# Ten instead of eight k-tiles of a hidden chunk through seven block products, their combinations seeded in PSUM

## The chip, the cores and the metric

The kernel runs on one core of one Trainium2 chip. A time is the device time of an execution in microseconds, and the median of several executions counts. The chip has five engines that matter here: TensorE (PE, matmuls), VectorE (DVE), ScalarE (ACT), GpSimd (POOL) and SyncE (SP, which issues most DMAs).

## What is computed

One layer of an encoder for 256 positions of width 2048: a half-step SwiGLU FFN, a combined attention of 16 heads with input and output projection, and a second half-step FFN. Only the first matrix product of the two FFNs is touched by the change:

```python
D_MODEL, SEQ, D_FF = 2048, 256, 5632

def swiglu_ffn(x, g, w_in, w_out):
    h = rms_norm(x, g)
    gate, up = jnp.split(h @ w_in, 2, axis=-1)
    return (jax.nn.silu(gate) * up) @ w_out

x = x + 0.5 * swiglu_ffn(x, ffn1_norm, ffn1_w_in, ffn1_w_out)
...
x = x + 0.5 * swiglu_ffn(x, ffn2_norm, ffn2_w_in, ffn2_w_out)
```

All data are float32, and the result has to be near float32.

## The kernel before

**Matmuls.** A float32 operand is split into a high part, rounded by ACT (`w_hi`, `h_hi`), and a low part, the rest, made by DVE (`w_lo`, `h_lo`). A product then takes three matmuls of 128 x 128 by 128 x 512: hi hi, hi lo, lo hi. Positions come in two tiles t of 128, the width 2048 in 16 k-tiles, the hidden width 5632 in 11 chunks of 512 (`NC`). Each chunk needs a gate and an up half of the weights.

**Units and the ring.** Weights land in `w_raw` (four slots of four k-tiles) or in the blocks `b_11`, `b_12`, `b_21`, `b_22`. They are used in units of two k-tiles (`UK`). Unit u is rounded by ACT into `w_hi[u % 4]` (`split_in_hi`, L963, counter `hi_ready`), DVE makes `w_lo[u % 4]` from it (`split_in_lo`, L1338, `lo_ready`), PE uses both (`units_used`). ACT waits for PE to be through with unit u-4 (`RING` = 4). ACT and DVE take their instructions in the order of the program, and so do their other duties, which are written out by hand between the units.

**Chunks.** The first chunk is computed plainly (16 units, gate in `acc[0]`, up in `acc[1]`). For the other ten (`IN_LOOPS`), 8 of the 16 k-tiles (`K_PLAIN`) are computed plainly and 8 through block products. The blocks are 2 x 2: the weights' k-tiles 8 to 11 and 12 to 15 by gate and up (`b_11`, `b_12`; `b_21`, `b_22`), the activations' position tiles by the same k-tiles. Seven products of 4 k-tiles (`KS`) take the place of eight:

- P1 = first activation block by `b_11`, P2 = second by `b_21`, P4 by the full sum `b_21` + `t_1`, P3 = fourth activation sum by `b_22`
- P5, P6 by `t_1` (the first sum `b_12 + b_11`, then the second sum `b_22 + t_1`), P7 by `b_12` after the third sum (`b_22 + b_12`)

DVE makes the three weight sums (`weight_sum`, L1353) and a DMA of POOL that accumulates adds `t_1` to `b_21` (L1909). The sums of the activations are made once per FFN (`activation_wide`, `signed_sums`, `split_sums`). P1, P6 and P7 go to the PSUM bank `partial[0]`, P5 to `partial[1]`. ACT copies P1 to `rows` (L1007), DVE adds P6, P7 and P5 there (L1411, L1447, L1449), and at the end of a loop adds the rows to `acc[0]` and `acc[1]` (L1411) before SiLU (L1047) and the gate product (L1465).

**Order of a loop on PE** (`hidden`): gate units G0, G0, G1, G1; eight transposes of the previous chunk's result (L570), which ACT copies to `act_raw` (L1012); P1, P5, an up unit, P2, an up unit, P6, P3, P7, P4, two up units. In all 8 plain units of 12 matmuls and 14 product units of 6. The loops are hardware loops over pairs of chunks on PE, ACT, DVE and SP (the last pair is written out on ACT and DVE).

**Beginning of the kernel.** SP issues x, the first chunk's weights, the blocks of the next one, a plain piece G0, then 17 small constants, then the other pieces. DVE runs `lambda_sums` (L1731 to L1733), which waits for these constants, behind the low parts of the first loop's G0 and G1 units, and after it the gate product of the first chunk (L1557).

## Time and profile before

| | us |
|---|---|
| median of 3 runs | 1803.63 (1803.62 to 1804.79) |
| the profiled execution | 1803.53 |
| its span in the profile | 1801.7 |
| PE, DVE, ACT busy | 1796.4, 1509.1, 1071.0 |

A row of the profile names engine, line, operation, output and inputs by the program's names. Times of a timeline count from the start of the span. A matmul's end is modelled, so that following matmuls overlap; their starts give the rate. SPq, PEld: the DMA issues of SyncE, the weight loads of TensorE.

### The profile page before, as it was taken

The page shows a single profiled execution, that of the slowest core. Times are in us where ns is not written, and L with a number is a line of the kernel's source. Part 1 is how long each engine was busy: PE and PEld are TensorE (multiplying, and loading weights), DVE is VectorE, ACT ScalarE, POOL GpSimd, SP SyncE. Part 2 cuts the span into 40 slices and gives each one's busy share as a digit, 9 for nine tenths or more (in the row PEclk, how much of TensorE's full clock was granted, in tenths as well). Part 3 has the DMA queues.
Part 4 walks back from the last instruction along what each step waited for, and adds up shares of the span by engine and source line. Part 5 has one row for each costly group of instructions (what it writes and reads, how often), then busy time and mean ns, then how long its engine had stood idle before and what let it go on. Part 6 is the DMA issues. An engine that isn't in the chain of part 4 may idle for free.

```text
span 1801.7 us, 22755 instructions
## 1 busy us (share of the span) xinstructions
PE 1796.4 (100%) x8227; PEld 1491.4 (83%) x8227; DVE 1509.1 (84%) x1594; ACT 1071.0 (59%) x1295; POOL 60.7 (3%) x93
## 2 busy tenths in 40 slices
PE   9999999999999999999999999999999999999999
...
PEclk9999999999999999999999999999999999999999
...
GB/s 359 235 238 233 234 230 210 221 222 186 164 169 251 188 220 212 197 171 164 164 164 187 143 166 182 257 222 224 235 238 240 227 232 237 127 187 164 238 206 141
DMA packets 181286, 372.92 MB, mean 207 GB/s; under 512 B 7504, under 2 KB 8544, under 8 KB 178400
## 3 DMA queue, kind: packets, MB, share of 16 engines
...
## 4 chain that ended last, share of the span: by engine, by line
PE 100%; DVE 0%; ACT 0%; POOL 0%; issue 0%; ACTq 0%; POOLq 0%
PE acc L539 14%; PE acc L541 14%; PE acc L540 13%; PE acc L601 8%; PE acc L599 8%; PE acc L600 8%; PE turn L612 4%; PE turn L613 4%; PE turn L614 4%; PE acc L612 3%; PE acc L614 3%; PE acc L613 3%; PE turn L570 1%; PE turn L716 1%; PE turn L715 1%; PE turn L714 1%
## 5 line engine op out<-in xcount | busy, mean ns | idle before, releaser
L1327 DVE TENSOR_TENSOR w_lo<-w_raw,w_hi 128x1024 fp32r<-128x1024 f32 x167 | 205.1, 1238 | 132.6 <-ACT w_hi L944 132.1
L944 ACT ACTIVATE w_hi<-w_raw 128x1024 fp32r<-128x1024 f32 x166 | 175.4, 1059 | 198.7 <-PE acc L541 177.1
L963 ACT ACTIVATE w_hi<-b 128x1024 fp32r<-128x1024 f32 x200 | 212.5, 1063 | 117.9 <-PE acc L601 76.1
L1338 DVE TENSOR_TENSOR w_lo<-b,w_hi 128x1024 fp32r<-128x1024 f32 x200 | 240.7, 1221 | 35.3 <-ACT w_hi L963 29.8
L977 ACT ACTIVATE w_hi<-w_raw 128x1024 fp32r<-128x1024 f32 x176 | 185.2, 1058 | 121.1 <-PE acc L541 87.8
L601 PE MATMUL acc<-w_hi,h_lo 128*128 128x512 f32 x640 | 249.1, 389 | 0.0
L599 PE MATMUL acc<-w_hi,h_hi 128*128 128x512 f32 x640 | 249.0, 389 | 0.0
L600 PE MATMUL acc<-w_lo,h_hi 128*128 128x512 f32 x640 | 249.0, 389 | 0.0
L1348 DVE TENSOR_TENSOR w_lo<-w_raw,w_hi 128x1024 fp32r<-128x1024 f32 x176 | 213.0, 1222 | 32.1 <-ACT w_hi L977 28.7
L963 ACT ACTIVATE w_hi<-w_raw 128x1024 fp32r<-128x1024 f32 x160 | 169.5, 1061 | 91.6 <-PE acc L601 64.1
L1338 DVE TENSOR_TENSOR w_lo<-w_raw,w_hi 128x1024 fp32r<-128x1024 f32 x160 | 191.9, 1220 | 28.8 <-ACT w_hi L963 26.2
L539 PE MATMUL acc<-w_hi,h_hi 128*128 128x512 f32 x496 | 196.4, 396 | 0.0
L541 PE MATMUL acc<-w_hi,h_lo 128*128 128x512 f32 x496 | 193.2, 390 | 0.0
L540 PE MATMUL acc<-w_lo,h_hi 128*128 128x512 f32 x496 | 193.1, 389 | 0.0
L539 PE MATMUL acc<-w_hi,act_hi 128*128 128x512 f32 x480 | 187.1, 390 | 0.0
L541 PE MATMUL acc<-w_hi,act_lo 128*128 128x512 f32 x480 | 186.8, 389 | 0.0
L540 PE MATMUL acc<-w_lo,act_hi 128*128 128x512 f32 x480 | 186.7, 389 | 0.0
L963 ACT ACTIVATE w_hi<-t 128x1024 fp32r<-128x1024 f32 x80 | 85.0, 1062 | 104.0 <-PE acc L601 98.1
L599 PEld LDWEIGHTS acc<-w_hi,h_hi 128*128 128x128 f32 x640 | 120.1, 188 | 25.1 <-DVE w_lo L1338 0.3
L601 PEld LDWEIGHTS acc<-w_hi,h_lo 128*128 128x128 f32 x640 | 120.1, 188 | 25.0
L600 PEld LDWEIGHTS acc<-w_lo,h_hi 128*128 128x128 f32 x640 | 120.1, 188 | 24.9
L539 PEld LDWEIGHTS acc<-w_hi,h_hi 128*128 128x128 f32 x496 | 93.1, 188 | 21.2 <-issue 2.7
...
## 6 DMA issues: line engine op xcount, KB each, us to landing
w_raw<-in_ffn_w_in SPq DMA_DIRECT2D x94, 1024.0 KB, 5.1
w_raw<-in_ffn_w_out SPq DMA_DIRECT2D x88, 1024.0 KB, 5.2
b<-in_ffn_w_in SPq DMA_DIRECT2D x80, 1024.0 KB, 5.3
w_raw<-in_w_in SPq DMA_DIRECT2D x48, 1024.0 KB, 5.0
b<-t POOLq DMA_DIRECT2D x20, 1024.0 KB, 8.3
w_raw<-in_w_out SPq DMA_DIRECT2D x16, 1024.0 KB, 4.9
...
```

The lines of the kernel that those rows point to most:

```text
L539: nc.tensor.matmul(o, hi, w_hi[:, slot, kk, :], start=first[t] and kk == 0, stop=False)
L540: nc.tensor.matmul(o, hi, w_lo[:, slot, kk, :], start=False, stop=False)
L541: mm = nc.tensor.matmul(o, lo, w_hi[:, slot, kk, :], start=False, stop=last[t] and kk == count - 1)
L599: nc.tensor.matmul(o, hi, w_hi[:, slot, kk, :], start=kk == 0 and not begun, stop=False)
L600: nc.tensor.matmul(o, hi, w_lo[:, slot, kk, :], start=False, stop=False)
L601: mm = nc.tensor.matmul(o, lo, w_hi[:, slot, kk, :], start=False, stop=stop and kk == UK - 1)
L944: nc.scalar.activation(w_hi[:, u % RING, 0:count, :], w_raw[:, slot, k0:k0 + count, :], ACT.Copy).then_inc(hi_ready, 1)
L963: nc.scalar.activation(w_hi[:, slot, :, :], in_raw(piece)[:, k0:k0 + UK, :], ACT.Copy).then_inc(hi_ready, 1)
L977: nc.scalar.activation(w_hi[:, u % RING, :, :], src, ACT.Copy).then_inc(hi_ready, 1)
L1327: nc.vector.tensor_tensor(w_lo[:, slot, 0:count, :], w_raw[:, v // 2 % RAW, k0:k0 + count, :], w_hi[:, slot, 0:count, :].bitcast(F32), ALU ...
L1338: nc.vector.tensor_tensor(w_lo[:, slot, :, :], in_raw(piece)[:, k0:k0 + UK, :], w_hi[:, slot, :, :].bitcast(F32), ALU.subtract).then_inc(l ...
L1348: nc.vector.tensor_tensor(w_lo[:, u % RING, :, :], src, w_hi[:, u % RING, :, :].bitcast(F32), ALU.subtract).then_inc(lo_ready, 1)
```

## The change

The number of k-tiles of a block product grows from 4 to 5 (`KS`), so 10 of the 16 k-tiles go through block products and 6 are plain. A product has three units, of 2, 2 and 1 k-tiles; a loop has 21 product units and 6 plain ones (`GA`, `GB`, `GC`, `UA`, `UB`, `UC`). The weight sums are single instructions over five k-tiles. The order of units is a list (`IN_ORDER`): P1, UA of the chunk before, P5, UB and UC of the chunk before, P2, transposes, P6, P7, P3, GA, GB, GC, P4.

The combinations start in PSUM: ACT copies P1 into `acc[0]` (`seed_p1`), P6 is accumulated onto P1 in `partial[0]`, DVE writes P5 minus that into `acc[1]` (`seed_c12`), adds P7 (`make_u3`), ACT copies it into `acc[0]` (`seed_u3`), DVE writes P5 minus it into `acc[1]` (`seed_c22`). The following units are accumulated on top, and SiLU and the gate read PSUM. Each DVE addition of a whole bank pair goes.

The hardware loops are written out on all engines. The accumulating DMA is issued in two parts. The SBUF is laid out anew (`t_1` lies over the fourth `w_raw` slot, the activation sums in `act_raw`). In the first FFN `lambda_sums` now stands before the first weight sum and the low parts of the first loop's P1 units. The blocks are loaded before G0 in both FFNs.

```diff
-KS = 4
+KS = 5
 K_PLAIN = KD - 2 * KS
 IN_LOOPS = FFN_ITERS - 1
-IN_PAIRS = IN_LOOPS // 2
 IN_FIRST = 16
 G0, G1, U0, U1, B11, B12, B21, B22, T1 = range(9)
-IN_RAW = ((G0, 0), (G0, 2), (G1, 0), (G1, 2), (B11, 0), (B11, 2), (T1, 0), (T1, 2), (U0, 0), (B21, 0), (B21, 2),
...
-IN_UNITS = len(IN_RAW)
-P1, P5, UP0, P2, UP1, P6, P3, P7, P4, UP2 = 4, 6, 8, 9, 11, 12, 14, 16, 18, 20
-SUM_OF = {P5: 1, P5 + 1: 1, P6: 3, P6 + 1: 3, P7: 2, P7 + 1: 2}
+PIECE_K = {G0: (0, 4), G1: (4, 2), U0: (0, 4), U1: (4, 2)}
+PIECE_SLOT = {G0: 0, G1: 1, U0: 2, U1: 1}
+PRODUCTS = {"P1": B11, "P5": T1, "P2": B21, "P6": T1, "P7": B12, "P3": B22, "P4": B21}
+PLAIN = {"GA": (G0, 0, 2, 0), "GB": (G0, 2, 2, 2), "GC": (G1, 0, 2, 4),
+         "UA": (U1, 0, 2, 4), "UB": (U0, 0, 2, 0), "UC": (U0, 2, 2, 2)}
 IN_SUMS = 3
-FREED = {G0: 2, G1: 4, B11: 6, U0: 12, B22: 16, B12: 18, B21: 20, U1: 22}
-assert 2 * IN_UNITS % RING == 0 and K_PLAIN == 2 * KT and IN_LOOPS == 2 * IN_PAIRS and KS == KT
+def loop_units(i):
+    up = {"P1": ("UA",), "P5": ("UB", "UC")} if i else {}
+    order = []
+    for name in ("P1", "P5", "P2", "P6", "P7", "P3", "GA", "GB", "GC", "P4"):
+        if name in PLAIN:
+            order.append((i, name) + PLAIN[name][:3])
+        else:
+            order += [(i, name, PRODUCTS[name], k0, min(UK, KS - k0)) for k0 in range(0, KS, UK)]
+        order += [(i - 1, plain) + PLAIN[plain][:3] for plain in up.get(name, ())]
+    return order
...
+            def load_loop(src, s_in, i):
+                later = i + 1 < IN_LOOPS
+                if later:
+                    load_in(src, s_in, i + 1, B11, LAST[i, "P1"])
+                if i:
+                    load_in(src, s_in, i, U1, LAST[i - 1, "UA"])
+                    load_in(src, s_in, i, U0, LAST[i - 1, "UC"])
+                if later:
+                    for piece, user in ((B12, "P7"), (B22, "P3"), (G0, "GB"), (G1, "GC"), (B21, "P4")):
+                        load_in(src, s_in, i + 1, piece, LAST[i, user])
...
+            def hidden(s_in, i, r0, n):
+                done = IN_LOOPS * n + i
+                up = i > 0
+                if i == 0 and s_in == IN2:
                     pe.wait_ge(bank_free[2], READS[s_in][2])
...
+                if done:
+                    pe.wait_ge(u2_copied, done)
+                form(s_in, i, "P1", block_of(0, 0), partial[0], True, False)
+                if up:
+                    pe.wait_ge(c22_seeded, done)
+                    plain_unit(s_in, i - 1, "UA", 1)
+                else:
+                    pe.wait_ge(s_ready, S_GROUPS * n + 1)
+                form(s_in, i, "P5", sum_of(1), partial[1], True, True)
+                if up:
+                    plain_unit(s_in, i - 1, "UB", 1)
+                    plain_unit(s_in, i - 1, "UC", 1, True)
+                pe.wait_ge(p1_seeded, done + 1)
+                form(s_in, i, "P2", block_of(1, 0), banks[0][:, 0, :], False, False)
+                turn_rows(r0 + i, 0, splits(r0), None, r0 + i)
+                form(s_in, i, "P6", sum_of(2), partial[0], False, True)
+                pe.wait_ge(turn_hi, r0 + i + 1)
+                form(s_in, i, "P7", sum_of(3), product[6], True, True)
+                pe.wait_ge(c12_seeded, done + 1)
+                form(s_in, i, "P3", sum_of(4), banks[1][:, 0, :], False, False)
+                pe.wait_ge(u3_seeded, done + 1)
+                for name in ("GA", "GB", "GC"):
+                    plain_unit(s_in, i, name, 0)
+                form(s_in, i, "P4", block_of(1, 1), banks[0][:, 1, :], False, True)
...
+            def seed_p1(s_in, n, i):
+                if i:
+                    act.wait_ge(gated, IN_LOOPS * n + i)
+                else:
+                    act.wait_ge(bank_free[0], READS[s_in][0] + 1)
+                act.wait_ge(units_used, UNIT[s_in] + IN_FIRST + LAST[i, "P1"] + 1)
+                nc.scalar.activation(acc[0][:, 0, :], partial[0], ACT.Copy).then_inc(p1_seeded, 1)
+            def copy_u2(s_in, n, i):
+                act.wait_ge(units_used, UNIT[s_in] + IN_FIRST + LAST[i, "P6"] + 1)
+                nc.scalar.activation(rows[:, 0, 0, :], partial[0], ACT.Copy).then_inc(u2_copied, 1)
+            def seed_u3(n, i):
+                act.wait_ge(u3_made, IN_LOOPS * n + i + 1)
+                nc.scalar.activation(acc[0][:, 1, :], rows[:, 0, 1, :], ACT.Copy).then_inc(u3_seeded, 1)
...
+            def hidden(s_in, s_out, i, r0, n):
+                ending = i == IN_LOOPS - 1
+                split_in_hi(s_in, n, LAST[i - 1, "P4"] + 5 if i else RING, LAST[i, "P1"] + 5)
+                seed_p1(s_in, n, i)
+                split_in_hi(s_in, n, LAST[i, "P1"] + 5, FIRST[i, "P6"] + 3)
+                copy_act(i, r0)
+                split_in_hi(s_in, n, FIRST[i, "P6"] + 3, LAST[i, "P6"] + 4)
+                copy_u2(s_in, n, i)
+                split_in_hi(s_in, n, LAST[i, "P6"] + 4, LAST[i, "P7"] + 5)
+                seed_u3(n, i)
+                if not ending:
+                    split_in_hi(s_in, n, LAST[i, "P7"] + 5, LAST[i, "P4"] + 5)
+                    silu(s_in, n, i)
+                    return
...
+            def first_sum(s_in, n, i):
+                done = IN_LOOPS * n + i
+                dve.wait_ge(lo_ready, UNIT[s_in] + IN_FIRST + (LAST[i - 1, "P6"] + 1 if i else 0))
+                dve.wait_ge(block_landed[B11 - B11], 16 * (done + 1))
+                dve.wait_ge(block_landed[B12 - B11], 16 * (done + 1))
+                if done:
+                    dve.wait_ge(full_sum_landed[0], 16 * done)
+                    dve.wait_ge(full_sum_landed[1], 16 * done)
                 weight_sum(t_1[:, :, :], b_12[:, :, :], b_11[:, :, :], ALU.add)
...
+            def third_sum(n, i):
+                dve.wait_ge(block_landed[B22 - B11], 16 * (IN_LOOPS * n + i + 1))
+                dve.wait_ge(sum_ready, SUMS * n + IN_SUMS * i + 1)
                 weight_sum(b_12[:, :, :], b_22[:, :, :], b_12[:, :, :], ALU.add)
...
+            def second_sum(s_in, i):
+                dve.wait_ge(lo_ready, UNIT[s_in] + IN_FIRST + LAST[i, "P5"] + 1)
                 weight_sum(t_1[:, :, :], b_22[:, :, :], t_1[:, :, :], ALU.add)
...
+            def seed_c12(n, i):
+                dve.wait_ge(rows_ready, ROWS[R_FFN2 if n else R_FFN1] + i + 1 - UNREADY)
+                dve.wait_ge(u2_copied, IN_LOOPS * n + i + 1)
+                nc.vector.tensor_tensor(acc[1][:, 0, :], partial[1], rows[:, 0, 0, :],
+                                        ALU.subtract).then_inc(c12_seeded, 1)
+            def make_u3(s_in, n, i):
+                dve.wait_ge(units_used, UNIT[s_in] + IN_FIRST + LAST[i, "P7"] + 1)
+                add(rows[:, 0, 1, :], product[6], rows[:, 0, 0, :]).then_inc(u3_made, 1)
+            def seed_c22(n, i):
+                dve.wait_ge(u3_made, IN_LOOPS * n + i + 1)
+                nc.vector.tensor_tensor(acc[1][:, 1, :], partial[1], rows[:, 0, 1, :],
+                                        ALU.subtract).then_inc(c22_seeded, 1)
+            def gate(s_in, n, i):
+                dve.wait_ge(units_used, UNIT[s_in] + IN_FIRST + LAST[i, "UC"] + 1)
+                dve.wait_ge(gated, IN_LOOPS * n + i + 1)
+                nc.vector.tensor_tensor(rows[:, 0, :, :], rows[:, 0, :, :], acc[1][:, :, :],
                                         ALU.mult).then_inc(rows_ready, 1)
+            def hidden(s_in, i, n):
+                if i:
+                    split_in_lo(s_in, LAST[i - 1, "P4"] + 1, FIRST[i - 1, "UA"])
+                    split_in_lo(s_in, FIRST[i - 1, "UA"], LAST[i - 1, "UA"] + 1)
+                    third_sum(n, i)
+                else:
+                    third_sum(n, i)
+                split_in_lo(s_in, FIRST[i, "P5"], LAST[i, "P5"] + 3)
+                second_sum(s_in, i)
+                if i:
+                    split_in_lo(s_in, LAST[i, "P5"] + 3, LAST[i - 1, "UC"] + 4)
+                    gate(s_in, n, i - 1)
+                    split_in_lo(s_in, LAST[i - 1, "UC"] + 4, LAST[i, "P6"] + 4)
+                else:
+                    split_in_lo(s_in, LAST[i, "P5"] + 3, LAST[i, "P6"] + 4)
+                seed_c12(n, i)
+                split_in_lo(s_in, LAST[i, "P6"] + 4, LAST[i, "P7"] + 4)
+                make_u3(s_in, n, i)
+                split_in_lo(s_in, LAST[i, "P7"] + 4, LAST[i, "GC"] + 1)
+                seed_c22(n, i)
+                if i + 1 < IN_LOOPS:
+                    first_sum(s_in, n, i + 1)
+                split_in_lo(s_in, FIRST[i, "P4"], LAST[i, "P4"] + 1)
...
-                    split_lo(s_in, 16, 20, PARTS_D)
                     lambda_sums()
...
+                first_sum(s_in, n, 0)
+                split_in_lo(s_in, 0, 3)
...
```

## Rows read from the trace of the kernel before

**Rows 1.** Page: busy time and share of engines; granted clock of PE in 40 slices.
```profile
PE 1796.4 (100%) x8227; PEld 1491.4 (83%) x8227; DVE 1509.1 (84%) x1594; ACT 1071.0 (59%) x1295; POOL 60.7 (3%) x93
...
PEclk9999999999999999999999999999999999999999
```

**Rows 2.** Timeline of PE, two loops' transposes: start, duration, line, operation, tiles, count.
```profile
274.21 0.40 PE L613 MATMUL turn<-w_lo,h_hi 128*128 128x512 f32 x1
274.44 0.39 PE L614 MATMUL turn<-w_hi,h_lo 128*128 128x512 f32 x1
...
314.80 1.03 PE L570 MATMUL turn<-cst,rows 128*128 128x128 f32 x8
...
315.90 0.40 PE L613 MATMUL turn<-w_lo,h_hi 128*128 128x512 f32 x1
```

**Rows 3.** Windows, one loop: length, PE, PEld, DVE, ACT, POOL busy, clock, DMA, GB/s.
```profile
273.90:315.60 41.70, 41.70 (x192) 34.63 (x189) 38.24 (x33) 25.93 (x27) 0.86 (x1) 1.00 0.71 226
```

**Rows 4.** Timeline of PE, ACT and DVE where a unit is released, last loop.
```profile
450.28 0.39 PE L612 MATMUL acc<-w_hi,h_hi 128*128 128x512 f32 x1
...
449.18 1.06 ACT L963 ACTIVATE w_hi<-t 128x1024 fp32r<-128x1024 f32 x1 [1.59 <-PE acc L601]
450.54 1.06 ACT L963 ACTIVATE w_hi<-t 128x1024 fp32r<-128x1024 f32 x1 [0.30 <-PE acc L614]
...
450.28 2.58 DVE L1338 TENSOR_TENSOR w_lo<-t,w_hi 128x1024 fp32r<-128x1024 f32 x2
```

**Rows 5.** Timeline where PE uses a low part at once: DVE, weight load, matmul.
```profile
466.59 2.35 DVE L1338 TENSOR_TENSOR w_lo<-w_raw,w_hi 128x1024 fp32r<-128x1024 f32 x2
...
467.86 0.19 PEld L599 LDWEIGHTS acc<-w_hi,h_hi 128*128 128x128 f32 x1 [0.16 <-DVE w_lo L1338]
...
467.96 0.39 PE L599 MATMUL acc<-w_hi,h_hi 128*128 128x512 f32 x1
```

**Rows 6.** Timeline of DVE, instructions issued back to back.
```profile
277.79 2.28 DVE L1353 TENSOR_TENSOR t<-b,t 128x2048 f32<-128x2048 f32 x1
279.99 2.35 DVE L1338 TENSOR_TENSOR w_lo<-b,w_hi 128x1024 fp32r<-128x1024 f32 x2
...
297.43 0.68 DVE L1447 TENSOR_TENSOR rows<-turn,rows 128x512 f32<-128x512 f32 x1
298.03 0.68 DVE L1449 TENSOR_TENSOR rows<-turn,rows 128x512 f32<-128x512 f32 x1
```

**Rows 7.** Timeline of DVE, low parts of a single k-tile at the kernel's beginning.
```profile
7.07 0.68 DVE L1837 TENSOR_TENSOR w_lo<-w_raw,w_hi 128x512 fp32r<-128x512 f32 x1
7.67 0.68 DVE L1840 TENSOR_TENSOR w_lo<-w_raw,w_hi 128x512 fp32r<-128x512 f32 x1
```

**Rows 8.** Timeline of PE and ACT: transposes, their copy, and roundings without a wait.
```profile
439.87 1.03 PE L570 MATMUL turn<-cst,rows 128*128 128x128 f32 x8
440.66 0.48 PE L612 MATMUL turn<-w_hi,h_hi 128*128 128x512 f32 x1
...
441.10 1.01 ACT L1012 ACTIVATE act_raw<-turn 128x1024 f32<-128x1024 f32 x1
...
464.70 1.99 ACT L963 ACTIVATE w_hi<-w_raw 128x1024 fp32r<-128x1024 f32 x2
```

**Rows 9.** Page, DMA issues: count, KB each, median us to landing.
```profile
b<-in_ffn_w_in SPq DMA_DIRECT2D x80, 1024.0 KB, 5.3
```

**Rows 10.** Kernel's beginning: window of all engines; timeline of POOL, DVE and PE.
```profile
20.00:30.00 10.00, 10.00 (x50) 8.38 (x49) 8.95 (x13) 9.90 (x22) 0.00 (x0) 1.00 1.05 408
...
51.87 0.09 POOL L1916 MEMSET gain_col<- 32x2 f32 x1 [50.47 <-DMA lam_in<-in_lambda_k]
...
57.70 0.29 DVE L1731 TENSOR_TENSOR lam_prod<-lam_in 128x128 f32<-128x128 f32 x1
...
58.47 1.23 DVE L1557 TENSOR_TENSOR rows<-acc,rows 128x1024 f32<-128x1024 f32 x1
...
53.75 0.39 PE L599 MATMUL acc<-w_hi,h_hi 128*128 128x512 f32 x1
```

More of the change, by code:

```diff
@@ L182, in hybrid_layer_kernel @@
         x_sb = sb("x_sb", [P, TT, D])
-        rows = sb("rows", [P, 2, TT, NC])
+        with ExitStack() as turned:
+            rows = sb("rows", [P, 2, TT, NC], F32, turned)
+        with ExitStack() as more:
+            sb("rows_gated", [P, TT, NC], F32, more)
+            s_lo_more = sb("s_lo_more", [P, 4, P], F32R, more)
+            s_hi_more = sb("s_hi_more", [P, 4, P], F32R, more)
+        sb("rows_room", [P, 2, TT, NC])
         with ExitStack() as gained:
@@ L358, in in_raw @@
             if piece < B11:
-                return w_raw[:, piece, :, :]
+                k0 = UK if piece == U1 else 0
+                return w_raw[:, PIECE_SLOT[piece], k0:k0 + PIECE_K[piece][1], :]
             return {B11: b_11, B12: b_12, B21: b_21, B22: b_22, T1: t_1}[piece][:, :, :]
-        def paired(i, half):
-            return lambda per, first=0: i * (2 * per) + (half * per + first)
         def turned_at(s):
@@ L426, in ffn @@
                     load_first(gate_up, s_in)
-                    load_in(gate_up, s_in, 0, True)
-                with sp.Fori(0, IN_LOOPS - 1) as i:
-                    load_in(gate_up, s_in, i)
+                    for piece in (B11, B12, B22, B21, G0, G1, U1, U0):
+                        load_in(gate_up, s_in, 0, piece)
+                for i in range(IN_LOOPS):
+                    load_loop(gate_up, s_in, i)
                 down = tiled(w2)
-                for slot in range(RAW):
-                    load(down, slot // 2 * NC, slot % 2 * KT, KT, slot, UNIT[s_out] - IN_UNITS + FREED[slot])
+                for slot, user in ((0, "GB"), (1, "UA"), (2, "UC"), (3, "P4")):
+                    load(down, slot // 2 * NC, slot % 2 * KT, KT, slot,
+                         UNIT[s_in] + IN_FIRST + LAST[IN_LOOPS - 1, user] + 1)
                 for m, (p, g, js) in enumerate(PERIODS[:N_LONG]):
@@ L598, in in_unit @@
                         o = banks[bank][:, t, :]
-                        nc.tensor.matmul(o, hi, w_hi[:, slot, kk, :], start=kk == 0 and not begun, stop=False)
-                        nc.tensor.matmul(o, hi, w_lo[:, slot, kk, :], start=False, stop=False)
-                        mm = nc.tensor.matmul(o, lo, w_hi[:, slot, kk, :], start=False, stop=stop and kk == UK - 1)
+                        nc.tensor.matmul(o, hi, w_hi[:, slot, kk, :], start=False, stop=False, skip_group_check=True)
+                        nc.tensor.matmul(o, hi, w_lo[:, slot, kk, :], start=False, stop=False, skip_group_check=True)
@@ L804, in ffn @@
                 hidden_first(s_in, r0)
-                with pe.Fori(0, IN_PAIRS) as i:
-                    for half in range(2):
-                        hidden(s_in, i, half, r0, n)
+                for i in range(IN_LOOPS):
+                    hidden(s_in, i, r0, n)
+                hidden_last(s_in, n)
                 down(s_out, r0, n, not final)
@@ L1096, in ffn @@
                     round_in_sums(n)
-                split_hi(s_in, 16, 20, PARTS_D)
-                with act.Fori(0, IN_PAIRS - 1) as i:
-                    for half in range(2):
-                        hidden(s_in, i, half, r0, n)
-                for half in range(2):
-                    hidden(s_in, IN_PAIRS - 1, half, r0, n, half == 1)
+                split_in_hi(s_in, n, 0, RING)
+                for i in range(IN_LOOPS):
+                    hidden(s_in, s_out, i, r0, n)
                 down(s_out, r0, n, final)
@@ L1421, in round_act @@
                                         ALU.subtract).then_inc(act_ready, 1)
-            def hidden(s_in, i, half, n, ending=False):
-                at = paired(i, half)
-                u0 = UNIT[s_in] + IN_FIRST
-                sums, copies, done = SUMS * n, 3 * IN_LOOPS * n, IN_LOOPS * n + 1
-                landed = at(16, (IN_LOOPS * n + 1) * 16)
-                dve.wait_ge(block_landed[B11 - B11], landed)
-                dve.wait_ge(block_landed[B12 - B11], landed)
+            def first_sum(s_in, n, i):
[6 more added lines that the diff above has]
+                    dve.wait_ge(full_sum_landed[1], 16 * done)
@@ L1557, in ffn @@
                 nc.vector.tensor_tensor(rows[:, 0, :, :], acc[1][:, :, :], rows[:, 0, :, :], ALU.mult).then_inc(rows_ready, 1)
-                with dve.Fori(0, IN_PAIRS - 1) as i:
-                    for half in range(2):
-                        hidden(s_in, i, half, n)
-                for half in range(2):
-                    hidden(s_in, IN_PAIRS - 1, half, n, half == 1)
+                for i in range(IN_LOOPS):
+                    hidden(s_in, i, n)
+                hidden_last(s_in, s_out, n)
                 down(s_out, r0, n, final)
```

312 lines of the change are left out of this document (150 added, 162 removed).

## The prediction

> **What bounds the kernel now.** I read the page first [rows 1]: TensorE (PE) is busy 1796.4 of 1801.7 us and its granted clock is full in all 40 slices, so there is no idle time to win and only fewer matmuls can shorten the run. A busy PE is one whose modelled spans overlap (one lasts 0.39 us), so the rate has to be read from starts. In the loop on the hidden chunks the starts lie 0.2267 us apart, and the second matmul after one group of eight transposes and the one after the next group are 41.69 us apart [rows 2]. That is 180 x 0.2267 = 40.81 plus 0.88 for the eight transposes and the late second matmul behind them (314.80 to 315.90 is 1.10, less the spacing). No stall is in it. The busy times of one loop [rows 3] then say who comes second: VectorE (DVE) 38.2 of 41.7 us, ScalarE (ACT) 25.9. So PE sets the pace with DVE close behind. Whether a loop can shrink depends on the ring of four rounded weight units: ACT rounds unit u only when PE has finished unit u-4, DVE then makes the low part, then PE may use it.
>
> **The links of that chain.** PE's next unit starts at 450.28 and ACT starts at 450.54, 0.26 later; the rounding started at 449.18 lasts 1.06, and DVE starts at 450.28, 0.03 behind its end [rows 4]. A low part lasts 1.22, and one ends at 467.81; the weight load starts at 467.86 and the matmul at 467.96, 0.16 later and just in time [rows 5]. From release to use: 0.26 + 1.06 + 0.03 + 1.22 + 0.16 = 2.73 us. Issued back to back DVE needs less per instruction: 2.20 for a sum of four tiles (277.79 to 279.99), 1.135 for two tiles (two in 2.35), 0.60 for one tile from PSUM [rows 6] or from SBUF [rows 7]. A sum of five tiles isn't in the trace: 2.20 + 0.53 (1.135 less 0.60 for one more tile) = 2.73, between 2.20 and twice 2.20.
>
> **What the change removes.** A loop has 8 plain units of 12 matmuls and 14 product units of 6 by the order in the code: 180. After it, 6 plain units and 7 products of 15 (units of 6, 6, 3): 177. Three matmuls fewer in 20 loops are 60 x 0.2267 = **13.6 us less**. Transposes stay. The unstalled loop takes 177 x 0.2267 + 0.88 = 41.01 us.
>
> **What DVE carries.** Before: 22 x 1.135 + 3 x 2.20 + 4 x 0.60 + 3 x 1.14 = 37.4. After: 20 x 1.135 + 7 x 0.60 + 3 x 2.73 + 3 x 0.60 (c12, u3, c22) + 1.14 (gate) = 38.0. It fits into 41.01. Seeding in PSUM saves the two wide adds, but 27 units and longer sums eat that. Writing PSUM from DVE isn't in the trace; I take the 0.60 of a PSUM read (bounds 0.35 to 1.1: half of it, and a two-tile instruction). ACT loses two full roundings and gains seven short ones and two copies of some 0.6: 25.9 - 2.1 + 4.2 + 1.2 = 29 of 41, not the bound.
>
> **Where the order stalls PE in an ordinary loop (i = 1 to 9).** I followed every wait of the new order. The three units between release and use last 3 x 1.36 = 4.08 us in products now (1.35 to spare) and 1.36 + 1.36 + 0.68 = 3.40 afterwards (0.67 to spare). Four places don't have enough:
> - P5. The low part of UA, the third sum and the low part of P5's first unit stand in this order on DVE. UA is released by the end of P4: 0.26 + 1.06 + 0.03 + 1.135 + 2.73 + 1.22 + 0.16 = 6.60. PE covers it with P1 and UA, 27 x 0.2267 = 6.12. Stall 0.48.
> - P7. ACT copies the transposes before it rounds P7's first unit. The last transpose ends 0.24 behind P6's first matmul; ACT starts at the earliest 0.10 later (the copy of before started 0.20 behind it, bound by its own queue), 0.93 for the copy, 1.04 for a rounding without a wait (two in 1.99) [rows 8], 0.03 + 1.22 + 0.16: 3.73. PE covers 15 x 0.2267 + 0.09 = 3.49. Stall 0.24.
> - P3 and GA. Between two such products DVE has 1.135 + 1.135 + 0.60 + 0.60 (c12, then u3) = 3.47 against PE's 3.40: 0.07 each, while DVE is behind.
> Everything else has room: P4 0.9 us behind the next first sum, P2 1.0 behind the second sum, the u3 seed 0.5. The sum is 0.86 us per loop, 18 loops: **15.5 us more** (bounds: 0.3, if both latencies are near zero, so that only half of P5's stall and little of P7's stay; 1.4, if a seed costs 1.1 instead of 0.60, which P3 then pays). So an ordinary loop takes 41.87, slower than 41.69. The B12 load (a four-tile load lands after 5.3 us [rows 9], five tiles about 6.6) is issued at P7's last low part and wanted by the first sum 8.6 us later: 2 to spare.
>
> **The first loop of each FFN** has no UA, UB, UC as cover. DVE queues the first chunk's gate, the third sum and P5's low part behind the end of the chunk: 0.26 + 1.14 + 2.73 + 1.22 + 0.16 = 5.51 against P1's 3.40: 2.1. P2's last unit stands behind the second sum, and that behind P2's middle unit, which is released when P5's first unit ends, 1.36 behind P5's start: 1.36 + 0.26 + 1.06 + 0.03 + 1.135 + 2.73 + 0.68 + 0.16 = 7.42 against 6.12 for P5 and two units of P2: 1.3. P6's rounding needs the same sum: its end is 0.6 ahead of P2's last unit, then 0.03 + 1.06 + 0.03 + 1.22 + 0.16 against 0.68 and the transposes: 0.3. P3 and GA: 0.1. **3.8 us more** in FFN2 (where the ordinary stall of P5 and P7 is not in loop 0).
>
> **FFN1 starts worse.** The lambda sums, which wait for the last of 17 small constant loads, now stand on DVE ahead of the first sum and of P1's low parts. Before, DVE did 57.70 to 58.47 with them when the landing (POOL resumes at 51.87) was long past. PE is through with the first chunk at 53.75. The loads queue behind the block loads, which the drain paces (408 GB/s from 20 to 30 us) [rows 10]; four blocks of 1.31 instead of 1.05 MB are 1.05 MB more, 2.6 us, so the landing is near 54.4. Then 0.77 + 2.73 + 1.22 + 0.16: P1 starts at 59.3 instead of 53.75, 5.5 late (3.0 if the loads are not shifted). P5 follows 3.3 late: from the start of P1's first low part DVE runs 1.135 + 1.135 + 0.60 + 1.14 + 2.73 + 1.22, + 0.16 = 8.12, PE starts P1 1.38 behind it and covers 3.40. Then 1.3 + 0.3 + 0.1 as above: **10.6 us more**. Small additions earlier (wider activation sums, about 1 us of DVE work) hide in this wait.
>
> Edits at nothing: unrolling of the loops, with no idle time at their boundaries now; the start of the down projection, whose first unit finds SiLU long done behind UA, UB, UC (8.2 us); the accumulating DMA in two parts, with 20 us before P4. Uncovered, each would cost below 2 us per FFN.
>
> **A rule against the change.** The granted clock is full throughout, but PE is idle for 5.3 us in the whole run [rows 1], less than the new wait alone. The Trainium skill (TensorE: Matmul & The Clock Gate, Part 1: The HAM clock gate) says that an idle array falls back to half rate. By it the product P1 of FFN1 would run at 1.2 GHz, and if its 15 matmuls took twice 0.2267 (an estimate) that is 3.4 us more, almost wholly under the 3.3 us for which P5 waits anyway.
>
> **Sum.** 15.5 + 3.8 + 10.6 - 13.6 = +16.3. The profiled run took 1803.53 (span 1801.7), the median is 1803.63: **1820 us**, +0.9%.
>
> **Rivals.**
> - Only the entries stall. If ACT and DVE run ahead more than I think, ordinary loops have their full gain: 1803.6 + 3.8 + 10.6 - 13.6 = 1804. For it: no stall today and two of my terms are 0.07. Against: P5's 6.60 to 6.12 comes from measured rows alone. Chance 0.13, no measurable change.
> - Faster: the ring hides nearly all of it, the loop stalls and most of the entries, and with 5 us of stalls in all the matmuls' gain gives 1803.6 + 5 - 13.6 = 1795, without any 1790. It decides below 13.6 us of stalls in sum. Chance 0.10.
> - Worse: one wait more in each loop. The seeds write the bank next to PE's, or B12 lands over 2 us late so that the first sum pushes P4; half a microsecond more in 20 loops is 10 us: 1830. It decides from 0.3 us per loop. The rule above belongs here, if the low clock outlasts P5's wait: 3 us more. Chance 0.2.
> - The forecast with its terms off by a third: 1810 to 1828. Chance 0.57.
> The change does what it says: the matmul count is arithmetic.
>
> **How the numbers follow.** About 0.2% (3.6 us) can be told from no change. Faster 0.10; same 0.13; slower 0.57 + 0.20 = 0.77. The range leaves out half of faster and the tail of worse: 1801 to 1832.
>
> **What would show it.** In the profile after: PE idle of about 5 us near 54 us, released by w_lo; loops 41.8 to 41.9 us apart; PE idle before P5's first unit (0.5) and P7's (0.2), released by DVE; 60 matmuls fewer; DVE busy near 95% in the loops. Loops of 41.0 would refute the queue argument; no idle time at 54 us, the constants' part. A slower P2, P4 or P6 would show a wait that I missed.

## The result and the profile after

The changed kernel takes **1828.79 us** (median of 4 runs, 1827.37 to 1830.44) against 1804.21 for the kernel before on the same chip: ratio 1.0135, 95% interval 1.0118 to 1.0153, 1.35% slower. Forecast were 1820 and a range of 1801 to 1832. The profiled execution took 1827.89 us with a span of 1826.1.

The page after, the lines that answer to [rows 1]:

```profile
span 1826.1 us, 21498 instructions
PE 1805.9 (99%) x8167; PEld 1477.5 (81%) x8167; DVE 1521.2 (83%) x1636; ACT 1120.4 (61%) x1437; POOL 78.9 (4%) x113
PEclk9999999999999999999999999999999999999999
```

60 matmuls fewer (8227 before), and yet a longer busy time: a waiting PE hardly shows in its share. So I went by the starts again. PE's timeline at two successive groups of transposes in FFN2, as in [rows 2]:

```profile
1348.52 1.03 PE L618 MATMUL turn<-cst,rows 128*128 128x128 f32 x8
...
1390.46 0.93 PE L618 MATMUL turn<-cst,rows 128*128 128x128 f32 x7
```

A loop of FFN2 takes 41.93 to 41.94 us (41.69 before, 41.87 forecast, 41.01 without stalls), one of FFN1 42.01 in the mean. All engines in one loop (columns as in [rows 3]): DVE is busy for 38.57 us, as forecast (38.0) and hardly more than before.

```profile
1348.50:1390.40 41.90, 41.67 (x186) 33.76 (x185) 38.57 (x35) 28.33 (x34) 1.78 (x2) 1.00 0.74 232
```

The wait ahead of P5, timelines of DVE (first three rows) and PE. UA's low part (1372.92), the third sum (1374.06, 2.82 us for five tiles) and P5's low part (1376.80) stand one behind the other; PE is through with UA and idle:

```profile
1372.92 1.23 DVE L1436 TENSOR_TENSOR w_lo<-w_raw,w_hi 128x1024 fp32r<-128x1024 f32 x1 [0.22 <-ACT w_hi L1041]
1374.06 2.82 DVE L1451 TENSOR_TENSOR b<-b 128x2560 f32<-128x2560 f32 x1
1376.80 2.95 DVE L1436 TENSOR_TENSOR w_lo<-t,w_hi 128x1024 fp32r<-128x1024 f32 x3
...
1377.46 0.39 PE L651 MATMUL acc<-w_hi,h_lo 128*128 128x512 f32 x1
1378.07 0.51 PE L665 MATMUL turn<-w_hi,s_hi 128*128 128x512 f32 x1 [0.23 <-DVE w_lo L1436]
1378.41 0.39 PE L667 MATMUL turn<-w_lo,s_hi 128*128 128x512 f32 x1
```

The bracket says 0.23, but a stall is read from the starts: 0.61 and then 0.34 where 0.227 is usual, 0.50 later in sum. The second matmul, behind the late one, starts late too. P7 in the same way (0.32 and 0.31, 0.18 in sum):

```profile
1352.65 0.39 PE L668 MATMUL turn<-w_hi,s_lo_more 128*128 128x512 f32 x1
1352.97 0.47 PE L665 MATMUL turn<-w_hi,s_hi 128*128 128x512 f32 x1
1353.28 0.40 PE L667 MATMUL turn<-w_lo,s_hi 128*128 128x512 f32 x1
```

The start of FFN1, which answers to [rows 10]: DVE, PE, and a window in which P1 runs. DVE waits 2.20 us for the constants, the first sum comes behind the lambda sums, and PE stands still from 54.6 to 60.28. In the window behind that the granted clock is 0.50 (1.2 of 2.4 GHz), and matmuls start 0.43 apart:

```profile
52.60 0.68 DVE L1647 TENSOR_TENSOR s_lo_more<-act_raw,s_hi_more 128x512 fp32r<-128x512 f32 x1
55.49 0.29 DVE L1866 TENSOR_TENSOR lam_prod<-lam_in 128x128 f32<-128x128 f32 x1 [2.20 <-DMA lam_in<-in_lambda_k]
...
56.27 2.83 DVE L1451 TENSOR_TENSOR t<-b 128x2560 f32<-128x2560 f32 x1
59.01 1.22 DVE L1436 TENSOR_TENSOR w_lo<-b,w_hi 128x1024 fp32r<-128x1024 f32 x1
...
54.39 0.39 PE L589 MATMUL acc<-w_hi,h_lo 128*128 128x512 f32 x1
60.28 0.80 PE L665 MATMUL turn<-w_hi,h_hi 128*128 128x512 f32 x1 [5.51 <-DVE w_lo L1436]
...
67.11 0.47 PE L665 MATMUL turn<-w_hi,s_hi 128*128 128x512 f32 x1 [0.83 <-DVE w_lo L1436]
...
60.20:65.20 5.00, 4.92 (x12) 3.90 (x13) 5.00 (x5) 1.06 (x1) 0.00 (x0) 0.50 0.42 127
```

The first loop of FFN2, PE's timeline at P5 and at P2's last unit (by the starts 2.2 and 1.3 us late):

```profile
1172.54 0.47 PE L665 MATMUL turn<-w_hi,s_hi 128*128 128x512 f32 x1 [1.95 <-DVE w_lo L1436]
...
1179.98 0.50 PE L665 MATMUL acc<-w_hi,h_hi 128*128 128x512 f32 x1 [0.99 <-DVE w_lo L1436]
```

**Where the time lies.** The groups of transposes cut a run into stages. Differences of their starts in the profiled executions, in us (the last two columns are runs of the next section):

| stage | before | after | e5 | e8 |
|---|---|---|---|---|
| start to FFN1's first group | 64.64 | 75.37 | 73.63 | 67.62 |
| nine loops of FFN1 | 375.23 | 378.10 | 377.78 | 369.52 |
| to the group of the down projection | 41.73 | 42.23 | 42.09 | 41.71 |
| down projection | 203.53 | 205.17 | 203.53 | 203.54 |
| attention, its projections, into FFN2 | 431.82 | 432.47 | 431.82 | 431.81 |
| to the first group in FFN2's loops | 44.41 | 47.46 | 48.08 | 45.34 |
| nine loops of FFN2 | 375.24 | 377.39 | 377.41 | 369.75 |
| to the group of the down projection | 41.73 | 42.19 | 42.09 | 41.74 |
| to the end | 223.39 | 225.67 | 224.55 | 223.80 |
| span | 1801.7 | 1826.1 | 1821.0 | 1794.8 |

I had forecast the rows with loops and first loops. **The two down projections and the attention, 1.64 + 2.28 + 0.65 = 4.6 us, stand nowhere in the prediction.** (Of the 2.28, 0.5 lies behind PE's last matmul.) The down projections run the same matmuls in the same order, and in this execution PE waits there no more than before. PE's instructions with the hidden activations, by line: number, then shortest, median and longest duration in ns, the kernel before first:

```profile
L540 PE MATMUL acc<-w_lo,act_hi x165: 389/389/389, 509.9 to 679.9; 128*128 128x512 f32 x165
```

and after:

```profile
L587 PE MATMUL acc<-w_hi,act_hi x164: 388/392/392, 510.3 to 679.6; 128*128 128x512 f32 x164
L588 PE MATMUL acc<-w_lo,act_hi x164: 392/394/394, 510.5 to 679.9; 128*128 128x512 f32 x164
```

Each matmul is a few ns slower; the starts lie up to 231 ns apart instead of 227. That is so only in products whose stationary operand is act_hi, act_lo, mix or a sum. With h it is 227 as before. The tiles act_hi, act_lo, mix and `s_hi` (the high parts of the sums) lie in SBUF behind the scratch tile `root`, which the change narrows from 88 to 72 elements (64 bytes): they start at a multiple of 512 bytes before and 64 bytes short of one after (act_hi at byte 137216 and 137152 of a partition). The change also moves `w_raw` behind `root`, so that all destinations of weight loads are 64 bytes off too.

### The profile page after: what moved, and what is told of

The parts are those of the page before. It is cut to its first block, busy times and chain, and to the rows that moved or that the text cites. A ratio compares the mean times of both kernels' runs of the same rounds, so it can differ in the third digit from the quotient of the medians.

```text
span 1826.1 us, 21498 instructions
## 1 busy us (share of the span) xinstructions
PE 1805.9 (99%) x8167; PEld 1477.5 (81%) x8167; DVE 1521.2 (83%) x1636; ACT 1120.4 (61%) x1437; POOL 78.9 (4%) x113
## 4 chain that ended last, share of the span: by engine, by line
PE 89%; DVE 6%; ACT 2%; issue 2%; SPq 1%; DMA 0%; POOL 0%; ACTq 0%; DVEq 0%; POOLq 0%
PE acc L587 13%; PE acc L588 13%; PE acc L589 13%; PE acc L649 5%; PE acc L651 5%; PE acc L650 5%; PE turn L665 4%; PE turn L667 4%; PE turn L668 4%; PE acc L665 3%; PE acc L668 3%; PE acc L667 3%; DVE b L1451 3%; ACT w_hi L1041 2%; DVE w_lo L1436 2%
## 5 line engine op out<-in xcount | busy, mean ns | idle before, releaser
L1041 ACT ACTIVATE w_hi<-b 128x1024 fp32r<-128x1024 f32 (+1 forms) x300 | 268.8, 914 | 145.3 <-PE acc L651 112.6
L1436 DVE TENSOR_TENSOR w_lo<-b,w_hi 128x1024 fp32r<-128x1024 f32 (+1 forms) x300 | 298.1, 1042 | 50.1 <-ACT w_hi L1041 47.6
L1426 DVE TENSOR_TENSOR w_lo<-w_raw,w_hi 128x1024 fp32r<-128x1024 f32 x159 | 195.2, 1238 | 123.7 <-ACT w_hi L1017 123.2
L1017 ACT ACTIVATE w_hi<-w_raw 128x1024 fp32r<-128x1024 f32 x158 | 166.9, 1059 | 189.5 <-PE acc L589 166.9
L1055 ACT ACTIVATE w_hi<-w_raw 128x1024 fp32r<-128x1024 f32 x184 | 193.9, 1059 | 140.0 <-PE acc L589 95.4
L1446 DVE TENSOR_TENSOR w_lo<-w_raw,w_hi 128x1024 fp32r<-128x1024 f32 x184 | 223.2, 1222 | 42.5 <-ACT w_hi L1055 38.9
L587 PE MATMUL acc<-w_hi,h_hi 128*128 128x512 f32 x496 | 196.4, 396 | 0.2 <-DVE w_lo L1426 0.2
L589 PE MATMUL acc<-w_hi,h_lo 128*128 128x512 f32 x496 | 193.3, 390 | 0.0
L588 PE MATMUL acc<-w_lo,h_hi 128*128 128x512 f32 x496 | 193.2, 390 | 0.0
L649 PE MATMUL acc<-w_hi,h_hi 128*128 128x512 f32 x480 | 186.9, 389 | 0.0
L650 PE MATMUL acc<-w_lo,h_hi 128*128 128x512 f32 x480 | 186.8, 389 | 0.0
L651 PE MATMUL acc<-w_hi,h_lo 128*128 128x512 f32 x480 | 186.8, 389 | 0.0
L1436 DVE TENSOR_TENSOR w_lo<-w_raw,w_hi 128x1024 fp32r<-128x1024 f32 x120 | 145.0, 1222 | 21.0 <-ACT w_hi L1041 20.5
L1041 ACT ACTIVATE w_hi<-w_raw 128x1024 fp32r<-128x1024 f32 x120 | 124.7, 1056 | 39.2 <-PE acc L651 22.0
L1041 ACT ACTIVATE w_hi<-t 128x1024 fp32r<-128x1024 f32 (+1 forms) x120 | 105.6, 917 | 67.8 <-PE acc L651 37.6
L1436 DVE TENSOR_TENSOR w_lo<-t,w_hi 128x1024 fp32r<-128x1024 f32 (+1 forms) x120 | 118.3, 1041 | 1.0 <-ACT w_hi L1041 1.0
L587 PEld LDWEIGHTS acc<-w_hi,h_hi 128*128 128x128 f32 x496 | 93.1, 188 | 22.1 <-issue 2.6
```

What stands on the lines that cost most here:

```text
L587: nc.tensor.matmul(o, hi, w_hi[:, slot, kk, :], start=first[t] and kk == 0, stop=False)
L588: nc.tensor.matmul(o, hi, w_lo[:, slot, kk, :], start=False, stop=False)
L589: mm = nc.tensor.matmul(o, lo, w_hi[:, slot, kk, :], start=False, stop=last[t] and kk == count - 1)
L649: nc.tensor.matmul(o, hi, w_hi[:, slot, kk, :], start=False, stop=False, skip_group_check=True)
L650: nc.tensor.matmul(o, hi, w_lo[:, slot, kk, :], start=False, stop=False, skip_group_check=True)
L651: mm = nc.tensor.matmul(o, lo, w_hi[:, slot, kk, :], start=False, stop=stop and kk == UK - 1, skip_group_check=True)
```

## The experiments

Each was timed in five rounds beside the kernel before, which took 1804.33 to 1804.63 us there. "Less" and "more" below are against the 1828.79 us of the changed kernel, which ran beside 1804.21; so they are good to some tenths of a us and the scatter of each median.

| run | edit to | median us | to before (95%) |
|---|---|---|---|
| e1_align | after: tiles 128 bytes short | 1837.81 | 1.0172 to 1.0199 |
| e2_before_shift | before: tiles 64 bytes short | 1811.50 | 1.0021 to 1.0048 |
| e3_third_dma | after: third sum by DMA | 1817.17 | 1.0056 to 1.0083 |
| e4_third_split | after: third sum split | 1821.11 | 1.0077 to 1.0105 |
| e5_align512 | after: tiles at 512 bytes | 1824.05 | 1.0094 to 1.0125 |
| e6_lambda_back | after: lambda sums later | 1827.66 | 1.0113 to 1.0144 |
| e7_copy_later | after: P7's rounding first | 1825.55 | 1.0101 to 1.0132 |
| e8_combo | e3 + e5 + e6 + e7 | 1798.24 | 0.9952 to 0.9979 |
| e9_combo_shifted | e8 without e5 | 1808.23 | 1.0012 to 1.0030 |
| e10_combo_pool | e8 + first sum by GpSimd | 1799.41 | 0.9962 to 0.9981 |

### Where the tiles start: e1, e2, e5

```
 e1 (after)                              e2 (before)
-root = sb("root", [P, 72])             -root = sb("root", [P, 88])
+root = sb("root", [P, 56])             +root = sb("root", [P, 72])
```

> The changed kernel with one scratch tile of VectorE 64 bytes narrower, so that all tiles behind it in SBUF (the hidden activations, the attention's activations, the rounded sums' high parts) start at a multiple of 128 bytes again, as in the kernel before; in the changed kernel they start 64 bytes off. Nothing else differs. In the changed kernel's trace matmuls whose stationary operand lies behind that tile start 229 to 232 ns apart, those with the normed input (h), which lies ahead of it, 226.8. Theory (the stationary operand's start address): act_hi and act_lo back from 229.0, 231.2 and 226.7 to 226.9, 227.0 and 226.3 in the down projections (3.8 us in both), the attention's output products 0.5 us, P5, P6, P7 and P3 in the loops from 230.4 to 232.7 back to 226.7 (at most 5 us, less where a wait for VectorE takes the room): 1819.5 to 1822 instead of 1828.8. Rival (the slow spacing is a trace left by the waits ahead of it, or by denser DMA traffic): the waits are the same, so the spacing and the time stay, 1828 to 1829.

> The kernel before with the same scratch tile 64 bytes narrower, so that the same tiles start 64 bytes off a multiple of 128. Theory (the address): the same matmuls as in the changed kernel go from 226.8 to 229 to 232 ns: 3.8 us in the two down projections, 0.5 in the attention's output, 960 matmuls with sums in the loops x 4 to 5 ns = 4 to 5 us. Loops 41.9 instead of 41.69 us, the whole 1812 to 1814 instead of 1804.2. Rival (waits or traffic): this kernel has neither more waits nor other traffic than before, so 1804.

e2 came as forecast in kind, smaller in size: 7.2 us slower, loops of 41.80 instead of 41.69 (41.9 expected), the same durations as after:

```profile
L540 PE MATMUL acc<-w_lo,act_hi x164: 394/394/394, 510.3 to 679.6; 128*128 128x512 f32 x164
```

Its starts lie 228.8 (w_hi with act_hi), 231.4 (w_lo with act_hi) and 226.5 ns (w_hi with act_lo) apart in the mean, in the down projections of after as well. `w_raw` and the moving operands w_hi and w_lo stay at multiples of 512 in e2: of all that these matmuls read, only the stationary operand has moved. In the profiled execution of e2 another 1.5 us lie in FFN1's first loop: ScalarE gets the second gate piece of weights 2.0 us later (rounding from 56.37 instead of 54.33), VectorE falls behind by as much, and PE waits for a low part. e1's forecast failed: 9 us slower instead of 7 to 9 faster. A multiple of 128 bytes isn't enough; 128 bytes short of a multiple of 512 is worse than 64 short, with starts 232.3 to 232.6 ns apart in the down projections for all three kinds. So e5 puts the six small tiles behind the large ones:

```
-sumsq, rstd, lam, root, gain_col, half_rstd ahead of w_raw
+sb("big_room", [P, 31232]), then the same six
```

> The changed kernel with its six small tiles of statistics and scratch allocated behind the large ones instead of ahead of them, so that the large tiles start at a multiple of 512 bytes, as in the kernel before (the changed kernel: 64 bytes short of one; the run with the narrower tile: 128 bytes short, all matmuls with these operands 232 to 234 ns apart and 9 us slower). Nothing else differs. Theory (the start address of the stationary operand within 512 bytes): act_hi, act_lo, mix and the sums back at 226 to 228 ns, 3.4 us less in the two down projections, 0.4 around the attention, 0.1 to 0.2 us in each loop: 1820.5 to 1823 instead of 1828.8, and the stretch from the last transposes of FFN1's loops to the first of the attention 203.5 instead of 205.2 us. Rival (what costs is not the address but some other feature that the two shifted kernels share): 1827 to 1830, the stretch at 205.2.

1824.05, 4.7 us less than after, where 5.8 to 8.3 were expected. The down projection took 203.53 as before, with this row for the products with act_hi:

```profile
L590 PE MATMUL acc<-w_lo,act_hi x164: 389/389/389, 510.3 to 679.6; 128*128 128x512 f32 x164
```

But the loops stayed at 41.93: the 0.24 us that the slow matmuls had cost in a loop went into waits for VectorE and matmuls a few ns late behind them, so VectorE sets the pace there. And the gain has a part that I had not looked for. While the start is bound by its loads, after and e5 moved (windows, last column GB/s; 408 before in [rows 10]):

```profile
20.00:30.00 10.00, 10.00 (x49) 8.35 (x49) 8.99 (x13) 9.88 (x22) 0.00 (x0) 1.00 1.05 388
```

```profile
20.00:30.00 10.00, 10.00 (x50) 8.35 (x49) 8.95 (x13) 9.89 (x22) 0.00 (x0) 1.00 1.05 409
```

The shifted destination costs 5% of the rate. In e2, where only the blocks are shifted and `w_raw` isn't, the window has 403; the other shifted kernels have 386 to 388. The last constants, which wait behind these loads, land at 53.75 instead of 55.46, and PE's P1 starts at 58.56 instead of 60.28 (59.84 to 61.02 in e1, e3, e4 and e7, which are shifted too). The Trainium skill (DMA: Bandwidth & Descriptors, How a descriptor splits into AXI transactions) tells of such a loss for what is read: a descriptor that doesn't start at a multiple of 256 bytes costs one transfer that begins at the multiple below. Here it is the destination that is off, so the two rows show a loss that the page doesn't state; no run here separates 256 from 512.

### VectorE's queue: e3, e4, e7

e3 (abridged; besides, ScalarE waits for P7 on the new semaphore, VectorE's third sum is deleted, and its second sum waits itself for B22's landing):

```
+pool.wait_ge(block_landed[B22 - B11], ...); pool.wait_ge(sum_ready, ...)
+for k in (slice(0, UK), slice(UK, KS)):
+    nc.gpsimd.dma_start(b_12[:, k, :], b_22[:, k, :], accum_op=ALU.add).then_inc(third_landed, 16)
```

> The changed kernel with the third weight sum (B22 + B12) taken from VectorE and made by two accumulating DMAs on GpSimd's queue, issued once the first sum is done and some 20 us before P7 wants it. Everything else as in the changed kernel, the misplaced tiles too. Theory of the prediction (P5 waits because VectorE has the third sum between UA's and P5's low parts): the 0.50 us ahead of P5 in 18 ordinary loops goes (9 us), in the first loop of FFN2 the 2.1 at P5 and most of the 1.15 at P2's last unit, in that of FFN1 most of the 1.0 at P5 and 1.15 at P2: 13 to 14.5 us less, 1814 to 1816. Rival 1 (P5 waits for the ring's latency, not for the sum): under 2 us less, 1827 to 1829. Rival 2 (1.3 MB of accumulating DMA more per loop delay the block loads): new waits for DMA, 1820 or more.

11.6 us less, below the 13 to 14.5 expected. Loops of 41.47 us make 9.1 in 18, the stages with the first loops of FFN1 and FFN2 another 1.5 and 2.1; no wait ahead of P5 is left. PE's timeline:

```profile
1338.26 0.93 PE L619 MATMUL turn<-cst,rows 128*128 128x128 f32 x7
...
1379.72 1.03 PE L619 MATMUL turn<-cst,rows 128*128 128x128 f32 x8
```

P2's last unit still waits 1.3 in each first loop, where I had expected most of that to go too: the second sum stands ahead of it, behind P2's middle unit, and that one's rounding waits for PE's release. The queue argument holds for P5. The DMA share rose from 0.74 to 0.91 of a loop without a new wait.

```
 e4
-weight_sum(b_12, b_22, b_12)                      # ahead of P5's low parts
+tensor_tensor(b_12[:, 0:3], ...)                  # there
+weight_sum(b_12[:, 3:KS], ...)                    # behind the low part that follows P5's
```

> The changed kernel with the third weight sum in two instructions: three tiles where the whole one stood, two tiles behind the low part of the unit after P5. VectorE's work is the same or 0.1 us more per loop. Theory: P5's wait of 0.50 goes (the queue ahead of its low part is 1.1 us shorter), but VectorE comes later to the second sum and P2's first low part, 0.15 us late there: 0.3 per loop and about 1 in each first loop less, 1821 to 1824. Rival (it is the amount of VectorE's work that counts, not where it stands): the wait moves to UB or P2 in full, 1828 to 1829.

1821.11, 7.7 us less, loops of 41.57, though VectorE does the same work in one instruction more: it is the place in the queue that costs, not the amount. The wait ahead of P5 is gone; PE waits about 0.1 us in P2's first unit instead. In e7 two ScalarE steps change places (abridged):

```
-split_in_hi(..., FIRST[i, "P6"] + 3); copy_act(i, r0)
+split_in_hi(..., FIRST[i, "P6"] + 4); copy_act(i, r0)
```

> The changed kernel with ScalarE rounding P7's first unit ahead of its copy of the transposed activations instead of behind it. Theory of the prediction (P7 waits because that copy stands ahead of its rounding): the wait of 0.09 and the late second matmul of 0.09 ahead of P7 go in all 20 loops, 3 to 4 us less, 1824.5 to 1826; loops of FFN2 41.75 instead of 41.93. Rival 1 (VectorE is full there, and the wait moves on to P3): 0 to 1 us less. Rival 2 (the copy, now later, keeps the bank that P7 writes): P7 waits for it instead, same or slower.

1825.55, 3.2 us less, loops of 41.75 to 41.81. P7's wait is where the prediction put it.

### The start of FFN1: e6

```
 split_sums(n)
-lambda_sums()                                     # ahead of first_sum
+lambda_sums()                                     # in loop 0, behind GC's low part
```

> The changed kernel with the lambda sums (three small VectorE operations that wait for the constants) moved from ahead of the first weight sum of FFN1 to the end of its first loop, behind GC's low part. Theory of the prediction: VectorE is free for the first sum at 53.3 instead of 56.3 us, P1's first matmul comes at 57.3 instead of 60.3 and P5's at 64.1 instead of 67.1: 3 us less, 1825 to 1827 with the scatter of the start. The clock: PE still sits idle for 3 us, so the rule of the clock gate makes P1 slow again; if it stays at full rate, P1 ends 2.4 us sooner, but P5 waits for VectorE just as long, so the whole stays the same. Rival (the first sum would have waited for the block loads anyway): no gain, 1828 to 1829.

PE's timeline has P1 at 57.23 and P5 at 64.06, as expected to 0.1 us:

```profile
54.46 0.39 PE L589 MATMUL acc<-w_hi,h_lo 128*128 128x512 f32 x1
57.23 0.50 PE L665 MATMUL turn<-w_hi,h_hi 128*128 128x512 f32 x1 [2.38 <-DVE w_lo L1436]
```

The first group of transposes comes 3.07 us earlier. The median gained only 1.1, which the scatter doesn't clearly exceed (the runs of e6 lie from 1826.3 to 1828.2, those of after from 1827.4 to 1830.4), so the start is shown by the timeline and not by the median. The profiled run, the fastest of e6, gained 1.6: it lost 0.6 us again in FFN2's loops (several took 42.0 instead of 41.93), for which I have no cause, and 0.8 in the down projections. Of these, 0.4 is a single wait at 1758 us, near the end. The profiled executions of e3, e5, e9 and e10 have it too (0.5 to 0.7 us), those of before, after and the others don't. In e5 the chain there leads to a load of w_out that took 8.5 us to land (median 5.2). After the idle time of 2.4 us the granted clock still fell to 0.50; P1's later matmuls start 0.427 apart, and P5 waits out the rest.

### All together: e8, e9, e10

> Four edits to the changed kernel at once: large tiles at multiples of 512 bytes, the third sum by accumulating DMAs, P7's rounding ahead of the copy, the lambda sums at the end of FFN1's first loop. If the causes add up as told (third sum 11.6 as measured, tiles 6 to 8, P7 3, lambda 3): 1802 to 1805, with loops of 41.05 to 41.15 us instead of 41.93, that is the unstalled loop of 41.01 that the prediction worked out; equal to the kernel before or up to 0.2% faster, since the first loops still lose 1.3 us in FFN2 and about 5 in FFN1. If a cause counted twice (the misplaced tiles hide in P7's wait): 1805 to 1809.

> The kernel with the four edits without the first of them: the small tiles stand ahead of the large ones again, which start 64 bytes short of a multiple of 512 as in the changed kernel. Theory (in the changed kernel the slow matmuls of the loops hid under VectorE's pace; with VectorE out of the way they show): loops 41.2 to 41.3 us instead of 41.04, 4 to 5 us in 20 loops, on top of the 4.7 us that the place of the tiles cost when it was the only edit: 1806.5 to 1808.5 instead of 1798.2. Rival (the costs simply add up): 4.7 us more, 1803.

e8: **1798.24 us, 0.35% faster than the kernel before** (0.21% to 0.48%). Its loop (PE's timeline, then the window of one loop):

```profile
1324.03 1.03 PE L621 MATMUL turn<-cst,rows 128*128 128x128 f32 x8
...
1365.09 1.03 PE L621 MATMUL turn<-cst,rows 128*128 128x128 f32 x8
...
1323.90:1365.00 41.10, 41.10 (x187) 34.09 (x186) 36.26 (x34) 28.45 (x34) 3.52 (x4) 1.00 0.91 269
```

41.04 to 41.06 us against 41.01 for the unstalled loop of the prediction, and 4 us below the 1802 to 1805 expected. The four edits alone gave 11.6 + 4.7 + 1.1 + 3.2 = 20.6 us, together 30.6. e9 shows where 5 of the other 10 are: with the waits gone, the tiles' place costs 10.0 us (1808.23) instead of 4.7. Loops of 41.25 against 41.04, with the stages to the down projections, are 4.1 of these; in the changed kernel this time was lost too, but under VectorE's queue. The start is the second place: its stage is 7.75 us shorter in e8, 6.3 in e3, e5 and e6 together. There PE idles only 0.59 us ahead of P1, and the granted clock stays full. The rest isn't settled.

e10 leaves VectorE's first sum in FFN1 to GpSimd (abridged; SyncE also waits for this sum before it loads the next B11):

```
+pool.wait_ge(lo_ready, UNIT[IN1] + IN_FIRST); ...
+nc.gpsimd.tensor_tensor(t_1[:, :, :], b_12[:, :, :], b_11[:, :, :], ALU.add).then_inc(sum_ready, 1)
```

> The kernel with the four edits and a fifth: the first weight sum of FFN1's first loop is made by GpSimd from 48 us on, while VectorE still works on the first chunk and the sums of the activations. Theory (in the first loop of FFN1 all waits of PE are for VectorE's queue): VectorE comes 2.8 us earlier to P1's low parts, PE's waits ahead of P1 (0.76), P5 (0.56) and P2's last unit (1.2) go or shrink, 1 to 2.5 us less than the 1798.2 of four edits: 1795.7 to 1797.2. Rival 1 (GpSimd is so slow that P5's rounding waits for it beyond 57.5 us, or it slows VectorE while it runs): 1798 to 1801.

Rival 1 came true: 1799.41, no gain. The profiled run (1801.60, one of the two slowest of ten) comes 4.3 us later to the first transposes than e8's. GpSimd's sum and the VectorE instruction beside it, which takes 2.29 us otherwise:

```profile
48.88 5.72 POOL L2058 TENSOR_TENSOR t<-b 128x2560 f32<-128x2560 f32 x1 [47.50 <-DVE w_lo L1431]
...
49.66 7.10 DVE L1645 TENSOR_TENSOR s_lo<-act_raw,s_hi 128x2048 fp32r<-128x2048 f32 x1 [0.91 <-ACT s_hi_more L1125]
```

VectorE ends 2.16 us after GpSimd does, about as long as its instruction takes alone: the rows look as if it did its work only then. The Trainium skill (SBUF — State Buffer, Terms, the entry on the shared port pair) says that VectorE and GpSimd lock each other out for a whole instruction; these rows, in which both read two tiles of SBUF, agree.

## Why the prediction was right, and where it wasn't

- **Removed work, 13.6 us less.** Right: 60 matmuls fewer, and e8's loops are 0.64 us shorter than before's, near the 0.68 of three matmuls.
- **P5, 0.48.** Right: 0.50, and it goes with the third sum (e3) or with its place (e4).
- **P7, 0.24.** 0.18 after, because PE came there later: its matmuls in P6, P7 and P3 lay up to 241 ns apart. In e5, with PE at full rate, the starts around P7 are 0.39 and 0.31 apart, 0.24 in sum; e7 confirms the cause. PE's timeline of e5:

```profile
1348.73 0.39 PE L670 MATMUL turn<-w_hi,s_lo_more 128*128 128x512 f32 x1
1349.12 0.47 PE L667 MATMUL turn<-w_hi,s_hi 128*128 128x512 f32 x1
1349.42 0.39 PE L669 MATMUL turn<-w_lo,s_hi 128*128 128x512 f32 x1
```

- **P3 and GA, 0.07 each.** Nothing after, for the same reason, and 0.03 and 0.04 in e5. In sum an ordinary loop of FFN2 took 41.93 instead of 41.87 in both. That is near, and in part by luck: after has 0.50 at P5, 0.18 at P7 and 0.24 in slow matmuls that the prediction didn't know. In FFN1 the nine loops took 42.01 (after) and 41.98 (e5) in the mean, one of them 42.21. All 18 took 1.8 and 1.5 us more than forecast.
- **First loop of FFN2, 3.8.** Right where it is large: P5 2.2 and P2 1.3, forecast 2.1 and 1.3. The stage is 3.05 longer with three matmuls fewer in it, 3.73, against 3.4 forecast in it. The 0.3 at P6, behind the transposes, isn't there.
- **FFN1's start, 10.6.** In its stage 9.4 net were forecast (P6 and the rest come later, three matmuls fewer); it was 10.73, and 8.99 in e5. The constants were forecast to land at 54.4 and P1 to start at 59.3: 55.46 and 60.28 after, 53.75 and 58.56 in e5. So the mechanism and its size were right without the slower DMAs. e6 shows the lambda sums' part, 3.05 us at P1 (2.20 of waiting, the rest their own work).
- **The clock rule.** P1 did run at half rate, its matmuls 0.427 apart where I took 0.453. P5's first matmul stands 6.83 behind P1's (forecast 3.40 + 3.3 = 6.7): the low clock hid wholly under P5's wait, so the sum by the row and the sum by the rule came to the same. In the changed kernel the 1.95 us of idle time in FFN2 lowered no clock; in e5 about the same wait did (0.50 from 1168.8 to 1172.2 us), and that stage took 0.6 us more. Behind 0.59 us (e8) it stayed full, behind 2.4 and 5.5 it fell.
- **The step that failed: "edits at nothing".** I listed unrolling, the down projection's first unit and the split DMA, and left out what the new layout of SBUF does to the addresses of everything behind the scratch tiles. A tile narrower by 64 bytes costs 4.7 us in the changed kernel (e5) and 7.2 in the kernel before (e2). The forecast of 16.3 more stands against 24.6 measured and 19.4 in e5. Of the remaining 3.1, 1.5 are the 18 loops; e5's profiled run shows 0.6 from the low clock in FFN2, 0.5 at the single wait of PE near the end (1755 us), and 0.5 more between PE's last matmul and the end. These last three I hadn't thought of.
- **The rivals.** The measured 1828.8 lies just above the 1810 to 1828 of "terms off by a third", and only the half of "worse" that the range took in kept it inside. 1830 for "worse" is the nearest number, but not by its mechanism: no wait of PE for a seed or for B12 stands in the trace. "Only the entries stall" and "faster" failed because ordinary loops do stall; e8, with the third sum, the copy, the lambda sums and the small tiles elsewhere, shows that "faster" was not far.
